# Second block's first mixer: indexer keys written to both halves of the array in turn, compressed keys transposed first, a part of the output product placed among the attention's last heads

## The reference, cut to what matters

```python
h = rms_norm(x, mix_norm[0])
q, c_kv, iq, ik, iw, q_mem = jnp.split(h @ a_w_in[0], A_SPLITS, axis=-1)
c_kv = rms_norm(c_kv, a_kv_norm[0])
# indexer: ik (256 x 64) against iq (8 heads x 64) gives scores; the best 64 keys of each query stay
rel = jax.nn.relu(jnp.einsum('bqhd,bsd->bqhs', iqb, ik) * (IDX_DIM ** -0.5))
# 12 heads: keys and values come from the compressed c_kv; softmax over the kept keys
seq_out = dsa_attention(q, c_kv, iq, ik, iw, a_w_uk[0], a_w_uv[0], rel_bias)
mem_out = memory_attention(q_mem, mem_n, w_mem_kv[0])      # 4 heads over 256 memory rows
x = x + jnp.concatenate([seq_out, mem_out], axis=-1) @ w_o[0]
x = x + peer_ffn(rms_norm(x, ffn_norm[0]), ...)            # gathers 128 rows of (u, v) per token
```

## Time and profile before

| | |
|---|---|
| Time of the kernel, three runs | 3128.9, 3129.5, 3137.11 us; median 3129.5 |
| The profiled execution | 3133.29 us, span 3131.5 us |
| PE busy | 2509.6 us, 80% |
| DVE busy | 1357.8 us, 43% |
| ACT busy | 859.5 us, 27% |
| POOL busy | 582.7 us, 19% |
| Moved by DMA | 1100.30 MB, mean 351 GB/s |
| Chain that ended last | PE 42%, DMA 39%, DVE 9%, issue 4%, ACT 4% |

### The profile page before, as it was taken

The page is one execution under the profiler, slowest core; times in us unless marked ns, Lnnn a source line. Parts: engine busy times, 40 slices in busy tenths (PEclk is TensorE's granted clock), DMA queues, the critical chain, the costliest instruction groups (busy, mean ns, idle before and its releaser), DMA issues.

```text
span 3131.5 us, 31191 instructions
## 1 busy us (share of the span) xinstructions
PE 2509.6 (80%) x10802; PEld 1309.1 (42%) x10802; DVE 1357.8 (43%) x3263; ACT 859.5 (27%) x2285; POOL 582.7 (19%) x558
## 2 busy tenths in 40 slices
PE   8998855657999766656788987798897989977776
PEld 6775311113777321212466532254452545522222
DVE  1352100001143201000174677768757787677764
ACT  0130000000122100000141433447533574344333
POOL 0000000000000000000011344434334334344442
PEclk9999878778999987888898999999999999999999
DMA  6336999999344699999623999999999999999997
GB/s 271 143 128 244 389 428 428 428 428 403 144 163 154 281 427 427 428 427 428 280 81 118 412 422 421 421 414 415 421 423 421 404 409 416 420 421 422 421 421 304
DMA packets 121196, 1100.30 MB, mean 351 GB/s; under 512 B 13488, under 2 KB 17360, under 8 KB 21968
## 3 DMA queue, kind: packets, MB, share of 16 engines
q1 hardware_dynamic: 45584, 558.26, 43.0%
q0 software_dynamic: 73728, 536.90, 41.4%
q10 hardware_dynamic: 1728, 3.14, 0.3%
HBM read 1094.06 MB, written 4.19 MB: 351 GB/s over the span
## 4 chain that ended last, share of the span: by engine, by line
PE 42%; DMA 39%; DVE 9%; issue 4%; ACT 4%; POOL 1%; SPq 0%; DVEq 0%; ACTq 0%; POOLq 0%
PE ps L668 24%; DMA wbuf<-in_puv,ar 18%; PE ps L1236 9%; DMA wbuf<-in_w_expert_up 8%; DMA wbuf<-in_w_expert_down 7%; PE ps L910 4%; DMA wbuf<-in_w_expert_gate 3%; DVE ar L1918 3%; ACT ar L1981 2%; PE ps L775 2%; PE ps L672 2%; DMA wbuf<-in_w_mem_kv 2%; ACT L1981 1%; PE ps L761 1%; DMA Y<-in_mem 1%
## 5 line engine op out<-in xcount | busy, mean ns | idle before, releaser
L1236 PE MATMUL ps<-wbuf,ar 128*128 128x512 f32 x2048 | 961.3, 608 | 220.5 <-ACT ar L1981 220.2
L1918 DVE CUSTOM_DVE_ANT_0 ar<-wbuf,Y 128x1024 f32<-128x1024 f32 x512 | 627.4, 1225 | 329.0 <-DMA wbuf<-in_puv,ar 320.4
L2465 POOL DMA_INDIRECT wbuf<-in_puv,ar x512 | 558.0, 1090 | 871.9 <-PE ps L1236 806.5
L910 PE MATMUL ps<-wbuf,ar 128*32 128x512 f32 x2944 | 457.5, 759 | 295.6 <-DMA wbuf<-in_w_expert_up 121.0
L1236 PEld LDWEIGHTS ps<-wbuf,ar 128*128 128x128 f32 x2048 | 366.7, 191 | 767.4 <-issue 765.0
L668 PE MATMUL ps<-HT,wbuf 128*128 128x256 f32 (+2 forms) x2784 | 510.6, 343 | 11.0 <-DVE HT L1265 3.4
L668 PEld LDWEIGHTS ps<-HT,wbuf 128*128 128x128 f32 (+1 forms) x2784 | 443.3, 194 | 76.8 <-issue 12.8
L1981 ACT ACTIVATE ar<-ar 128x1 f32<-128x1 f32 (+2 forms) x1052 | 270.1, 257 | 653.7 <-DVE ar L1918 626.4
L910 PEld LDWEIGHTS ps<-wbuf,ar 128*32 128x32 f32 x2944 | 94.7, 125 | 640.0 <-issue 200.3
L2449 POOL TENSOR_TENSOR sm<-sm,co 128x1 f32<-128x1 f32 (+1 forms) x18 | 10.3, 573 | 1608.4 <-DVE sm L1271 1599.1
L1978 ACT COPY ar<-ps 128x512 f32<-128x512 f32 (+2 forms) x123 | 69.0, 561 | 627.0 <-PE ps L910 305.4
(11 more groups left out here) (146 smaller groups left out, 1495.0 us busy)
## 6 DMA issues: line engine op xcount, KB each, us to landing
wbuf<-in_w_expert_down SPq DMA_DIRECT2D x64, 2048.0 KB, 26.4
wbuf<-in_w_expert_up SPq DMA_DIRECT2D x62, 2048.0 KB, 26.0
wbuf<-in_w_expert_gate SPq DMA_DIRECT2D x58, 2048.0 KB, 26.0
wbuf<-in_w_in SPq DMA_DIRECT2D x22, 2048.0 KB, 10.7
wbuf<-in_peer_w_q SPq DMA_DIRECT2D x12, 2048.0 KB, 11.3
wbuf<-in_w_o SPq DMA_DIRECT2D x6, 2048.0 KB, 10.7
wbuf<-in_b_w_in SPq DMA_DIRECT2D x6, 2048.0 KB, 11.4
wbuf<-in_w_branch_b SPq DMA_DIRECT2D x4, 2048.0 KB, 12.2
```

Source lines behind the costliest of these rows:

```text
L910: m = T.e.matmul(ps(jobs[n])[32 * k:32 * k + 32, :], lhs(c, k), v[:, 512 * n:512 * n + 512], start=(c == 0), stop=(c == 7), tile_position= ...
L1236: m = T.e.matmul(acc[n][:, :], DG[:, j % 4, :], rows_of(name)[:, 1024 + 512 * n:1536 + 512 * n], start=(j == 0), stop=(j == 127))
L1918: V.did(V.e.tensor_tensor_reduce(JK, rows_of(f"g{l}{i}.{j}")[:, 0:1024], Y[:, i, :], 1.0, 0.0, ALU.mult, ALU.add, DT[:, i, j:j + 1]), f"do ...
L2465: G.land(G.e.indirect_dma_start(out=rows_of(name), out_offset=None, in_=I["puv"], in_offset=bass.IndirectOffsetOnAxis(ap=IX[:, i, j:j + 1] ...
```

## The change

Three things change, all in the first mixer of the second block.

1. The 16 matmuls of `ma.ik` were eight for partitions 0 to 63, then eight for 64 to 127. Now the two halves alternate chunk by chunk, each with its tile position.
2. In the tensor and the scalar program the first step of `dense()` (transposes of the compressed keys, and their copy) is taken ahead of the memory's attention. All further steps of side work in the memory's attention move up by one unit.
3. `out_product` moves out of `prep_both`, remembers which chunks a job has had, and is called after steps 8 to 13 of the attention: two chunks each time, alternating between `ma.r00` and `ma.r10` as `ahead` lists, with the two banks kept. `prep_both` is unchanged and issues only what is left.

```diff
+            def out_product(half, i, chunks, keep=False):
+
+                job = f"ma.r{half}{i}"
+                v = tile(f"ma.wo{half}")
+                if job not in given:
+                    given[job] = [keep]
+                    take(job, keep)
+                todo = [c for c in chunks if c not in given[job][1:]]
+                for c in todo:
+                    T.wait_ge(*at["mm.o.out" if c > 5 else f"ma.os{c // 2}.out"])
+                    m = T.e.matmul(ps(job)[:, :], aOT[:, c, 128 * i:128 * i + 128], v[:, c, :],
+                                   start=(len(given[job]) == 1), stop=(len(given[job]) == 8))
+                    given[job].append(c)
+                if todo and len(given[job]) == 9:
+                    T.did(m, job, *([f"ma.wo{half}.used"] if i else []))
+                    if given[job][0]:
+                        release(job)
...
-                for a in (0, 64):
-                    m = mm(b[a:a + 64, 0:256], [(v[:, c, 0:64], HT[:, c, :]) for c in range(8)])
+                for c in range(8):
+                    for a in (0, 64):
+                        m = T.e.matmul(b[a:a + 64, 0:256], v[:, c, 0:64], HT[:, c, :], start=(c == 0), stop=(c == 7),
+                                       tile_position=(0, a))
...
                 side = dense()
+                next(side)
                 T.wait_ge(*at["ma.qm.out"])
                 T.wait_ge(*at["mem.v11.out"])
                 T.wait_ge(*at["mem.v10.out"])
                 for n, _ in enumerate(attend("mm", with_bufs(mem_units("mm", 0, aQM, 2), tb_a, pb_a), 2)):
-                    if n < 5:
+                    if n < 4:
                         next(side)
                 T.wait_ge(*at["ma.q0.out"])
+                ahead = {8: (0, 0, (6, 7)), 9: (0, 0, (0, 1)), 10: (1, 0, (6, 7)), 11: (1, 0, (0, 1)),
+                         12: (0, 0, (2, 3)), 13: (1, 0, (2, 3))}
                 for n, _ in enumerate(attend("ma", with_bufs(a_units(), tb_a, pb_a), 2)):
                     next(side, None)
...
+                    if n in ahead:
+                        out_product(*ahead[n], True)
...
                 side = dense()
+                next(side)
                 for n, _ in enumerate(attend("mm", with_bufs(mem_units("mm", 0, aQM, 2), tb_a, pb_a), 2, 3)):
-                    if 0 < n < 6:
+                    if 0 < n < 5:
                         next(side)
```

More of the change, by code:

```diff
@@ L956, in experts @@
                 drain(extra)
+            given = {}
+            def out_product(half, i, chunks, keep=False):
[14 more added lines that the diff above has]
+                        release(job)
             def mix_a():
```

## The result

The changed kernel takes 3114.26 us (median of four runs, 3112.65 to 3115.55), against 3130.66 us for the kernel before, measured beside it (median of four runs, 3128.9 to 3137.11). The ratio is 0.9938, with a 95% interval of 0.9927 to 0.9950. The forecast was 3114, in a range of 3106 to 3128. The profiled execution took 3115.55 us, with a span of 3113.8 us, 17.7 us less than before.

What follows compares the result with a forecast made beforehand. PE's chain to the first gather was taken as the bound, with a fixed 1400 us of full-rate transfers behind. Gains 2.8 + 6.0 + 6.8 = 15.6 us off the 3129.5 median gave 3113.9, range 3106 to 3128.

Steps and rivals of the forecast that it cites:

- An earlier mixer ends the kernel earlier by as much: From mixer to kernel end: each microsecond the mixer ends earlier starts transfers and moves the end one microsecond earlier.
- hidden-gain rival: Transfers behind the first gather: starting earlier, they run into something fixed, giving 3129 us; chance 0.04.
- Part 1: Indexer keys: alternating column halves overlap, so 32 records take 3.8 us; saving 2.8 us, bounds 0 to 3.4.
- Part 2: Memory's attention: taking compressed keys' transposes and copy first saves 6.0 us, bounds 2.0 to 6.2.
- 3.78 from the wait, and 3.68 - 1.89 = 1.8 because `ma.kt0` no longer runs at half clock: PE before and in ma.kt0: ACT's earlier copy removes a 3.78 us wait and 1.8 us of half clock.
- rival that DVE sets the pace behind: After the memory's attention: DVE limits the compressed-keys gain to 2.0 us, 11.6 us in all, 3118; chance 0.04.
- Part 3: Attention's end: twelve output products moved among the last units fill waits and restore full clock, saving 6.8 us.
- Waits filled: Attention's last units: moved products fill PE's waits of 0.92, 1.08, 0.41 and 0.82 us, gaining 3.2 us.
- clock's terms: Attention's end: first pair at half clock costs 1.7 us; full clock behind gains 5.3, and 0.8 in old first products.
- a clock that never falls: Attention's end: if the clock never falls there, another 3 us, so the moved products win 9.8 us.
- rival with the clock at half throughout: Attention's end: half clock through all six pairs makes the products' term -7.2 us; total gain 1.6, 3128; chance 0.13.
- slower one built on it: Attention's end and behind: half clock also through the twelve later products and following dense run, giving 3145 us; chance 0.04.

Runs made afterwards that it cites:

- e7: Changed kernel with two ma.r01 products ahead of those waiting for the last heads, and the first four product pairs one step earlier; 3110.30 us, ratio 0.9929.
- e4: Kernel before with the 16 indexer-key matmuls done twice over; ratio to the kernel before 1.0016.
- e12: Kernel before with only the compressed keys' transposes and their copy taken first, other side work at its old unit; ratio 0.9993.
- e8: Changed kernel with the queries ma.q0 behind the transposes of memory unit 2 again; ratio to the kernel before 0.9957.
- e2: Kernel before with only the compressed-keys-first edit, including side work moved up one unit; ratio 0.9976.
- e3: Kernel before with only the twelve output products moved among the attention's last units; ratio 0.9975.
- e10: The changed kernel run again, unaltered; 3115.74 us, ratio to the kernel before 0.9948.
- e5: Changed kernel with tile positions kept but indexer keys not alternating, eight matmuls per half in turn; ratio to the kernel before 0.9959.
- e9: Changed kernel with three pairs of output products among the last units instead of six; ratio to the kernel before 0.9952.

## Why the prediction was right

**An earlier mixer ends the kernel earlier by as much: right.** Over all 14 profiles the time from the first gather to the end of the span lies between 1430.5 and 1432.9 us, while the gather itself moved by 27 us, from 1673.32 (e7) to 1700.56 us (e4). The hidden-gain rival is out.

**Part 1: right in mechanism, mis-sized by what the clock does behind it.** The keys take 3.67 us (forecast 3.8) and 6.3 without alternation, so they give 2.6 of the 2.8 us. The Trainium skill, "TensorE: Matmul & The Clock Gate", Part 3 ("What overlaps and what doesn't"), says that a weight load overlaps a matmul in flight only across row groups. The trace does not agree: the 32 loads of 0.137 us in the changed kernel are 4.4 us together, and loads and matmuls are done in 3.67 us. What the term left out stands right behind: the weights and compressed keys took 14.0 us in five kernels without alternation and 12.4 in e4, against 10.7 us in five kernels with it and 12.4 in three. The windows of the kernel before and of the change over this stretch:

```profile
1549.70:1563.70 14.00, 14.00 (x65) 12.19 (x64) 0.60 (x2) 0.37 (x1) 0.00 (x0) 0.76 0.01 1
```

```profile
1546.10:1556.70 10.60, 10.60 (x66) 9.54 (x64) 0.60 (x2) 0.37 (x1) 0.00 (x0) 1.00 0.27 114
```

The same records, at a granted clock of 0.76 and of 1.00. No kernel with alternation had the long stretch at half clock there, nor had any kernel without it (e4 included) the stretch at full clock throughout. Why is not settled: the part shifts this stretch in time as well, and no run separates the shift from the denser work. In the profile after, 1.5 us of it were given back at half clock ahead of the memory's scores. That, with the 0.8 us at the start, the 1.1 us at the end and 0.5 us more from parts 2 and 3, is why 17.7 us were measured where 15.6 were summed. In the medians it is 16.4 us. That these lie so close to 15.6 is in part luck: the clock's share of part 1 was not in the sum, and half clock elsewhere took some of it back.

**Part 2: right in size (6.0 forecast, 6.3 measured), wrong in its account, so the size is luck.** The step "3.78 from the wait, and 3.68 - 1.89 = 1.8 because `ma.kt0` no longer runs at half clock" credits the copy's early start. e12 shows that the copy alone gives 2.6 us, since PE meets its next wait, for DVE, 2.6 us after it begins `ma.kt0`. The other 3.7 us come from `ma.q0` one unit earlier (e8), for which I had only noted the cost: DVE's wait for the transposes of unit 2 (1.5 us forecast, 1.05 measured, in DVE's timeline of the changed kernel):

```profile
1590.38 0.69 DVE L1276 COPY ar<-ps 128x512 f32<-128x512 f32 x1 [1.05 <-PE ps L672]
```

That cost was indeed absorbed, and the rival that DVE sets the pace behind is out: e2 has the full 6.3 us.

**Part 3: right in mechanism, 7.0 us against 6.8.** In the first profile the clock came back after the first pair and the value products, as the sum assumed; the new wait for the last heads was 0.86 us (0.8 forecast). Waits filled less the new one are 2.5 us (2.4 forecast), and the clock's terms 4.5 us (4.4 forecast). e3 gives the same by itself. How much half clock is left was luck: from the transposes of unit 6 to those of tile 0 it is 6.0 and 5.5 us in these two profiles, 3.4 in e8 and e10, and none in e5. The stretch is then 32.2, 32.0, 30.9, 31.0 and 29.4 us, so the same products win 7.0 to 9.8 us, and the 9.8 is what the forecast gave for a clock that never falls. That the products are what keeps the clock is clear even so: half clock takes 17 to 21 us of the stretch in the five profiles without them, and 0 to 6 us in the nine with them. The rival with the clock at half throughout, and the slower one built on it, did not show in any of these nine. e9 splits the two gains in another way: at full clock the waits would have been 4.0 us and not 3.2, and the clock's share, with no less waiting than before, is at least 4.8 us.

## What to carry to other kernels

A wait that ends earlier is worth only the distance to the next wait on the same engine: go through the queue behind it, and place other work ahead of that next wait too. Where PE runs at half clock among short waits, a few dense matmuls in between can be worth more than the gaps that they fill (here 4.5 us of clock and 2.5 us of gaps). Two groups of matmuls in different column halves run side by side over their whole length only if they alternate in program order. And before a step's gain is put down to the step, look where half clock fell in each profile: it moved the end of this attention by up to 2.8 us between profiles with the same order there.

## What the runs showed of the hardware

- Two groups of eight matmuls in different halves, one after the other, take 6.3 us for 32 records, and four such groups 11.6 us, where I had expected 6.8 and 13.6. Neighbouring groups overlap at each change of half: a group of 16 records takes 3.67 us by itself, but in e4 the next one starts each time 2.65 us behind it (records at 1539.12, 1541.77, 1544.42 and 1547.06 us), ahead of its last three records.
- Half clock came during a stretch in which PE was busy without a gap: the window from 1549.7 to 1563.7 us above, of whose 64 records the first 32 have 8 columns and the others 256. The clock was full for the same records in the changed kernel. A busy PE does not by itself keep the full clock. Nor does a wait of 2.65 us by itself lose it (e5).
- The time ahead of the mixer differs by up to 8 us between profiled runs (first projection at 1524.3 to 1532.2 us), with the same instructions ahead of it. From the first gather to the end they differ by 2.4 us only, so the mixer and what lies ahead of it hold most of what differs between these profiles.
